# A down projection by seven half-depth products for each pair of output tiles, with sums of weights and activations on the vector engine

## The reference

```python
def conv_ffn(h, buf, w_up, cw, cb, w_down):
    z = h @ w_up
    gate, up = z[..., :D_FF], z[..., D_FF:]
    gg = jnp.concatenate([buf, gate], 1)
    gc = dwconv_valid(gg, cw) + cb
    return (jax.nn.silu(gc) * up) @ w_down, gg[:, -(FFN_CONV_WIDTH - 1):]
...
    f, ffn_state = conv_ffn(rms_norm(x, ffn_g), ffn_buf, w_up, fcw, fcb, w_down)
    return x + f, conv_state, ffn_state
```

## Time and profile before

| | |
|---|---|
| median of 3 runs | 2145.61 us (2143.18 to 2148.26) |
| the profiled execution: its own time, its span | 2146.83 us, 2145.0 us |
| mean granted TensorE clock | 0.959 of full speed |
| PE busy | 2032.3 us, 95% of the span |
| DVE busy | 1154.1 us, 54% |
| ACT, POOL busy | 365.6 us, 113.5 us |
| DMA | 200.23 MB, mean 93 GB/s |
| chain that ended last, by engine | PE 90%, DVE 6%, ACT 3% |

### The profile page before, as it was taken

The page is one execution under the profiler, slowest core; times in us unless marked ns, Lnnn a source line. Parts: engine busy times, 40 slices in busy tenths (PEclk is TensorE's granted clock), DMA queues, the critical chain, the costliest instruction groups (busy, mean ns, idle before and its releaser), DMA issues.

```text
span 2145.0 us, 26339 instructions
## 1 busy us (share of the span) xinstructions
PE 2032.3 (95%) x9926; PEld 1567.8 (73%) x9926; DVE 1154.1 (54%) x2762; ACT 365.6 (17%) x957; POOL 113.5 (5%) x219
## 2 busy tenths in 40 slices
PE   8999779999999999999999988799989999999999
PEld 5767656777777777777776677567767777777777
DVE  4997566554066666600069974755431767765000
ACT  1012156212110000100000121652221100000000
POOL 1002030000000000000000020300000000000000
PEclk9998679999999999999999986899999999999999
DMA  6203262652312222111231022226522122221112
GB/s 249 73 0 91 79 206 76 219 186 95 106 57 73 73 75 77 70 65 54 93 129 63 1 88 69 74 100 190 185 106 89 50 79 79 79 79 51 63 72 71
DMA packets 109985, 200.23 MB, mean 93 GB/s; under 512 B 13698, under 2 KB 81555, under 8 KB 104611
## 3 DMA queue, kind: packets, MB, share of 16 engines
q1 hardware_dynamic: 103618, 167.01, 23.6%
q0 software_dynamic: 5568, 30.39, 4.0%
q10 hardware_dynamic: 672, 1.16, 0.2%
HBM read 190.82 MB, written 15.94 MB: 96 GB/s over the span
## 4 chain that ended last, share of the span: by engine, by line
PE 90%; DVE 6%; ACT 3%; issue 1%; DMA 0%; POOL 0%; DVEq 0%
PE ps L908 26%; PE ps L536 18%; PE ps L689 9%; PE ps L549 9%; PE ps L579 8%; PE ps L977 2%; PE ps L861 2%; PE ps L735 2%; PE ps L521 2%; PE ps L807 1%; PE ps L766 1%; PE ps L674 1%; PE ps L595 1%; PE ps L752 1%; PE ps L618 1%
## 5 line engine op out<-in xcount | busy, mean ns | idle before, releaser
L536 PE MATMUL ps<-rC,rB 128*128 128x288 f32 x1056 | 257.1, 406 | 0.0
L536 PEld LDWEIGHTS ps<-rC,rB 128*128 128x128 f32 x1056 | 200.6, 190 | 55.4
L1395 DVE SCALAR_TENSOR_TENSOR catT<-XC,par,catT 128x512 f32<-128x512 f32 x240 | 180.4, 752 | 8.3
L1811 DVE TENSOR_TENSOR xT<-xT,ps 128x576 f32<-128x576 f32 x14 | 10.6, 754 | 289.2 <-PE ps L536 250.9
L908 PE MATMUL ps<-catT,rD 128*128 128x288 f32 x528 | 131.6, 406 | 0.0
L689 PE MATMUL ps<-WR,rD 128*128 128x254 f32 x512 | 120.7, 393 | 0.0
L908 PEld LDWEIGHTS ps<-catT,rD 128*128 128x128 f32 x528 | 100.3, 190 | 27.7
L908 PE MATMUL ps<-catT,XC 128*128 128x288 f32 x480 | 119.8, 406 | 0.4 <-DVE rD L1766 0.4
L908 PE MATMUL ps<-rA,WR 128*128 128x288 f32 x448 | 117.8, 406 | 0.0
L689 PEld LDWEIGHTS ps<-WR,rD 128*128 128x128 f32 x512 | 99.9, 197 | 16.6 <-issue 0.3
L908 PEld LDWEIGHTS ps<-catT,XC 128*128 128x128 f32 x480 | 91.0, 190 | 26.2 <-issue 1.2
(11 more groups left out here) (304 smaller groups left out, 3215.0 us busy)
## 6 DMA issues: line engine op xcount, KB each, us to landing
WR<-in_w_up SPq DMA_DIRECT2D x56, 512.0 KB, 3.6
rB<-in_w_down SPq DMA_DIRECT2D x16, 1408.0 KB, 6.1
WR<-in_kvc SPq DMA_DIRECT2D x128, 128.0 KB
rB<-in_ksT SPq DMA_DIRECT2D x256, 64.0 KB, 1.9
rB<-in_w_up SPq DMA_DIRECT2D x32, 512.0 KB, 4.4
rD<-in_kvc SPq DMA_DIRECT2D x96, 128.0 KB, 2.2
WR<-in_w_glu SPq DMA_DIRECT2D x16, 512.0 KB, 5.4
WR<-in_w_out SPq DMA_DIRECT2D x16, 512.0 KB, 3.5
```

Source lines behind the costliest of these rows:

```text
L536: ins = mm(ps[:, bank + hf, 0:HN], w[:, k * P:(k + 1) * P], rhs[:, k, hf * HN:(hf + 1) * HN], start=k == 0, stop=k == K - 1)
L1395: stt(yc[:, 0:SEQ], xc[:, k:k + SEQ], w, yc[:, 0:SEQ], ALU.mult, ALU.add)
```

## The change: what it does

The 2 x 2 scheme of seven products, which `expand` has, is applied to the down projection. Two output tiles (a pair q = 0 to 3) and the two halves of the tokens make the four outputs, the 22 tiles of depth are cut into two times 11 (`FH`), and each of seven products p1 to p7 is 11 matmuls into one bank: 77 for a pair in place of 88. DVE makes four sums of weights for each pair (s1 to s4, 11 tiles of 128 columns each, into `WR` and `XC`) and four sums of activations for each layer (t1 to t4, 11 tiles of 288 columns each, into `rA`, `catT`, `XC`, and t2 in place in `actT`). The products are added to `xT` with broadcasts: a1 to four quarters of the pair, a6 to three, a5 and a7 to two, a2, a3 and a4 to one.

Both tiles of a pair lie in one buffer, `rB` for pairs 0 and 2, `rD` for pairs 1 and 3 (`DW`). So a pair is loaded as 2 x 1408 KB when the pair two before it is done. As `rB` is now filled whole for pair 0, its second tile covers ring slots 4 and 5, and the last step of `expand` takes slots 0 and 1 (`up_slots`), those of step 19, two steps before it. The next layer's `w_glu` tiles are fetched in the last pair, when `WR` is free again. In layer 0 the last pair runs in the order p1, p2, p7, p6, p4, p5, p3, and the second tile's right half is squared before the first's.

Core of the diff:

```diff
+        DW = [rB[:, :].rearrange("p (h f n) -> p h f n", h=2, f=FT), rD[:, 8192 - 2 * FT * P:8192].rearrange("p (h f n) -> p h f n", h=2, f=FT)]
...
+        def up_slots(f):
+            return (0, 1) if f == FT - 1 else ((2 * f + 4) % 6, (2 * f + 5) % 6)
...
             def up_ring(l, n):
-                s = (n + 4) % 6
+                s = up_slots(n // 2)[n % 2]
                 seen_of["unit_made"] += 1
                 if n >= 2:
-                    sp.wait_ge(sh["unit_made"], seen_of["unit_made"] - 6)
+                    sp.wait_ge(sh["unit_made"], seen_of["unit_made"] - (6 if n // 2 < FT - 1 else 3 + n % 2))
...
-                sp.wait_ge(sh["unit_made"], seen_of["unit_made"])
+                sp.wait_ge(sh["unit_made"], seen_of["unit_made"] - 2)
                 down(l, 1)
+                sp.wait_ge(*count("act_done", FT))
...
+                sp.wait_ge(*count("ff_out", 16))
                 for m in range(2, KD):
-                    sp.wait_ge(sh["down_made"], l * KD + m - 1)
+                    if m >= 4 and m % 2 == 0:
+                        sp.wait_ge(sh["down_made"], 28 * l + 7 * (m // 2 - 1))
                     down(l, m)
...
+                def product(bank, w, h, each=None):
+                    for k in range(FH):
+                        if each:
+                            pe.wait_ge(*count(each))
+                        ins = mm(ps[:, bank, 0:HN], w(k), h(k), start=k == 0, stop=k == FH - 1)
+                    ins.then_inc(sh["down_made"], 1)
...
+                    def p5():
+                        after(ahead + 3, ds=1, dt=1)
+                        product(2, lambda k: DS1[:, k], lambda k: DT1[:, k])
...
+                    pe.wait_ge(*count("wb_in" if q % 2 else "wa_in", 32))
+                    p1()
+                    if q and not last:
+                        square_sum(2 * q - 2, 6, sq2, KD)
+                    p2()
...
+                    if q < 3 or last:
+                        p5()
+                        p7()
+                        p6()
+                        p3()
+                        p4()
...
+                dve.wait_ge(sh["act_done"], FT * (l + 1))
+                t1()
+                s1(0)
+                t3()
+                s3(0)
+                t2()
+                s2(0)
...
+                    if q == 0:
+                        s4(0)
+                        t4()
+                    a5(())
+                    if q < 3:
+                        s1(q + 1)
+                    a7()
+                    if q < 3:
+                        s3(q + 1)
+                    a6()
+                    if q < 3:
+                        s2(q + 1)
```

More of the change, by code:

```diff
@@ L54 @@
 FO_W = FWD - (FW - 1)
+FH = FT // 2
 KVB = NH * HD
@@ L252, in build @@
         names = ("x_in0 x_in1 x_in2 x_in3 const_in pages_in const_ok idx_made setup par_in hist_in w1_in uc_out "
[L253 removed]
+                 "wr_in0 wr_in1 wr_in2 wr_in3 wr_in4 wr_in5 wd_in0 wd_in1 zw_in2 zw_in3 unit_made z_made z_kept down_made wa_in wb_in dt_made ds_made d_added sq_made sq_summed mu_made "
                  "var_made std_made h_made glu_gate glu_done conv_made mu_taken "
@@ L341, in _ @@
             for l in range(DEPTH):
+                if l:
+                    for ch in range(2):
+                        qkv(l, ch)
                 for s in range(4):
+                    if l and s % 2 == 0:
+                        sp.wait_ge(sh["down_made"], 28 * l - (1 if s else 3))
                     ring(s, I["w_glu"][l, s])
[L344 to L349, removed]
+                if l == 0:
+                    for ch in range(2):
+                        qkv(l, ch)
+                else:
+                    sp.wait_ge(sh["down_made"], 28 * l)
                 sp.dma_start(rD[:, 4096:8192], I["w1"][l]).then_inc(sh["w1_in"], 16)
@@ L968, in contract @@
                 last = l == DEPTH - 1
-                for m in range(KD if last else KD - 2):
-                    pe.wait_ge(*count(f"wd_in{m % 2}", 16))
-                    if m >= 2:
-                        pe.wait_ge(*count("x_upd"))
[L973 to L983, removed]
@@ L1002, in _ @@
+                if last:
+                    pe.wait_ge(sh["d_added"], 28 * DEPTH)
             for k in range(6):
@@ L1282, in expand, with squares @@
                 act.wait_ge(*count("act_done", 2))
-            def squares(ready, left=None, right=None):
+            def squares(ready, left=None, right=None, order=(6, 7)):
                 def half(k, hf):
@@ L1301, in squares @@
                 if right:
-                    right(6)
-                half(6, 1)
+                    right(order[0])
+                half(order[0], 1)
                 root(nrs[:, 0:HN])
                 if right:
-                    right(7)
-                half(7, 1)
+                    right(order[1])
+                half(order[1], 1)
                 act.wait_ge(*count("sq_summed", 4))
@@ L1723, in contracted @@
                 dve.wait_ge(*count("down_made"))
-                add_half(7, 3, 1)
+                step(tt(xT[:, 6, HN:NT], xT[:, 6, HN:NT], ps[:, 4, 0:HN], ALU.add))
+                dve.sem_inc(sh["x_upd"], 1)
+                dve.sem_inc(sh["d_added"], 1)
             def weight_sums(f):
-                wg, wu = ring6[(2 * f + 4) % 6], ring6[(2 * f + 5) % 6]
+                wg, wu = [ring6[s] for s in up_slots(f)]
                 w = WS[f % 2]
@@ L1806, in contract @@
                 last = l == DEPTH - 1
-                for m in range(KD if last else KD - 2):
-                    dve.wait_ge(*count("down_made"))
[L1809 to L1815, removed]
-                    dve.wait_ge(*count("down_made"))
-                    add_half(6, 1, 1)
+                b11, b12 = actT[:, 0:FH, 0:HN], actT[:, 0:FH, HN:NT]
@@ new lines, in s1, with s3, s2 @@
+                def s1(q):
+                    dve.wait_ge(*count("wb_in" if q % 2 else "wa_in", 32))
+                    w = DW[q % 2]
+                    tt(DS1, w[:, 1, 0:FH], w[:, 1, FH:FT], ALU.add).then_inc(sh["ds_made"], 1)
+                def s3(q):
+                    w = DW[q % 2]
+                    tt(DS3[0], w[:, 0, 0:10], w[:, 1, 0:10], ALU.subtract)
+                    tt(DS3[1], w[:, 0, 10:FH], w[:, 1, 10:FH], ALU.subtract).then_inc(sh["ds_made"], 1)
+                def s2(q):
+                    dve.wait_ge(sh["ds_made"], 16 * l + 4 * q + 2)
+                    tt(DS2, DS1, DW[q % 2][:, 0, 0:FH], ALU.subtract).then_inc(sh["ds_made"], 1)
@@ new lines, in s4, with add @@
+                def s4(q):
+                    dve.wait_ge(sh["ds_made"], 16 * l + 4 * q + 3)
+                    w = DW[q % 2]
+                    for i, (a, b) in enumerate(((0, 4), (4, 8), (8, FH))):
+                        ins = tt(DS4[i], w[:, 0, FH + a:FH + b], DS2[:, a:b], ALU.subtract)
+                    ins.then_inc(sh["ds_made"], 1)
+                def add(x, bank, n=1):
+                    src = ps[:, bank, 0:HN]
+                    if n > 1:
+                        src = src.unsqueeze(1).to_broadcast([P, n, HN])
+                    step(tt(x, x, src, ALU.add))
```

152 lines of the change are left out of this document (122 added, 30 removed).

## The result

The changed kernel takes 2109.61 us (median of 4 runs, 2108.4 to 2110.98) beside 2144.69 us (4 runs, 2143.18 to 2148.26) for the kernel before. The ratio is 0.9834, 95% interval 0.9817 to 0.9851: 35 us faster, between 32 and 39.

A forecast was written before the change was run, and what follows sets the result against it. PE, busy 95% of the span, was taken as the bound. Matmuls removed (-42.7), the final add (-0.3) and step 21 (+14.2) gave -28.8 us against the 2145.6 us median: 2116.8 us, range 2110 to 2125.

The forecast's parts named there:

- Matmuls removed: Down projection: 88 fewer matmuls over both layers at 0.485 us each, a gain of 42.7 us.
- DVE's sums: Down projection: DVE's sums of weights and activations stay hidden behind PE's products, even at a layer's start; cost 0.
- The loads: Down projection: loads of each pair's two weight tiles land before PE wants them, pair 0 with little to spare; cost 0.
- The weights of step 21: Last up-projection step: PE waits 4.8 us for late-issued weights, then loses 2.3 us to half clock; 14.2 us for both layers.
- Between the layers: From the last pair to the next layer's first product: the shorter cover of PE work still suffices; cost 0.
- the end: Last layer: the final add has 288 columns instead of 576, 0.3 us better.
- PE starts at 907.2 and its clock is at half until 911: Start of the down projection, after the POOL wait: half clock costs about 1.9 us.
- rival (b): The clock falls less, or the step 21 loads land sooner: 2112 to 2114 us; chance 0.07.
- (a): DVE's sums are late: 2139 us at double their time, 2120 to 2126 for small shortfalls; chance 0.11.
- (c): Slower than before: pair loads become the bound, 2168 us at 50 us a landing; chance 0.02 with others of its sign.
- (d): The change moves nothing: the scheme's products would have to run at 0.53 us a matmul; chance 0.02.

The follow-up runs named there:

- the late tile: Changed kernel, but step 21 keeps ring slots 4 and 5; pair 0's second tile loads after it, awaited behind p2: 2097.56 us, later 2100.01 us.

## Why the prediction was wrong

- **Matmuls removed, 42.7 us: right.** 5.33 us for 11, PE busy for 120.00 of 120.00 us.
- **DVE's sums, 0: right.** t1 took 3.46 us (3.5 said), s1 1.62 (1.6). s1 was made 1.6 us ahead of p5, and the run with t1 made three times shows that this margin is all there is. I had said 3 us, because I had PE at half clock there.
- **The loads, 0: right.** w_down landed after 5.8 to 9.5 us, and no product waited for it.
- **The weights of step 21, 14.2 us: right, a little small.** The two shifts are 7.5 and 7.4 us, 0.7 us over the sum. The wait was 4.95 us and half clock cost 2.1 us in the first product and 0.4 in the next. The Trainium skill's fit ("SBUF — State Buffer", "The DMA setup-cost knee") gives, as an estimate for the two loads as one megabyte, 4.4 us. The waits for them were 4.75 to 5.19 us in the twelve layers that have one, so it was short; the measurement decides.
- **Between the layers, 0, and the end, 0.3: right.** No wait of PE from 911 to 1110.
- **The failed step: "PE starts at 907.2 and its clock is at half until 911", taken over into the changed kernel as a fixed cost that stands in both sums.** The wait of 2.0 us did stay, as I wrote, and the half clock behind it went, in both layers, 1.7 us each (my 1.9 counted as clock the 0.2 us that every group shows on top); it also went behind the 2.2 us wait of layer 1's `project`, 1.7 us. I had counted the clock where I added a wait and not where I moved one. The gain is 6.3 us above the forecast of 28.8 (and before came out 0.9 us lower here, which makes the time 7.2 us lower), and this is 5.1 us of it. The step's size of 7.5 for 7.1 takes 0.7 us back, so 1.9 us are left, whose cause I cannot name. That is within what the same kernel varies by: the medians of before here run from 2142.1 to 2145.9 us, and the time ahead of step 21, which the change does not touch, by 4.5 us over the fourteen profiles.
- **The range** reached down to 2110 with rival (b), "the clock falls less", which was the right kind of miss, but I priced it at the new wait alone, and there the clock fell as forecast. Rivals (a), (c) and (d) did not come.

## What to carry to other kernels

In this kernel a shift of a few microseconds changed which of the short waits behind it are followed by half clock, in both directions. So a forecast of a change that moves work should leave some 2 us in the range for each wait of 2 to 3 us behind it, gain and loss alike. When a buffer is taken over for a bigger tile, ask which part is read first: here loading the second half late, behind the products that do not read it, saved the wait of 4.9 us on step 21 and 10 to 12 us in all. A scheme that trades an eighth of the matmuls of a product for sums on an idle engine kept its whole gain here, because the first sums fit beside products that need none; the margin there was 1.6 us and is the first thing to check.

## What the runs showed of the hardware that I had not expected

The granted clock behind a wait of 2.0 us was a matter of when it fell: half for 8 of 8 unmoved waits in the kernels without the 4.9 us wait, full for 8 of 8 in those with it, and reversed by a shift of 1.94 us in layer 0 of both. It repeated in the second profile of before, of the changed kernel and of that with the late tile. Elsewhere it did not always: the wait of 3.2 us at 18 to 21 us was followed by half clock in some profiles of a kernel and not in others, and the rest of layer 1 took 793.4 and 796.9 us in the two profiles of the kernel with the late tile. The fourteen waits of 4.75 to 5.3 us at step 21 and before p5 were followed by half clock each time, with 1.9 to 3.0 us lost. Products of float32 ran at 0.485 us a matmul beside DVE sums that read and wrote the same buffers, with no loss to be seen (120.00 of 120.00 us busy, 11 matmuls in 5.33 us).
